# Stick-breaking attention of a hybrid decoder step: products of sigmoids by a scan, instead of log sums by matmuls

## The reference, cut to what matters

```python
z = jnp.einsum('bqhd,bkhd->bhqk', q, k, preferred_element_type=jnp.float32) * (SB_HEAD_DIM ** -0.5)
z = z + sb_bias.astype(jnp.float32)[None, :, None, None]
causal = k_pos[None, :] < q_pos[:, None]
log_keep = jnp.where(causal, jax.nn.log_sigmoid(-z), 0.0)
log_a = jax.nn.log_sigmoid(z) + lax.cumsum(log_keep, axis=3, reverse=True) - log_keep
a = jnp.where(causal, jnp.exp(log_a), 0.0)
return jnp.einsum('bhqk,bkhd->bqhd', a, v.astype(jnp.float32)).astype(v.dtype)
```

## Time and profile before

| | |
|---|---|
| median of 3 runs | 1183.52 us (1182.88 to 1184.49) |
| the profiled execution | 1182.75 us, its span 1181.0 us |
| TensorE matmuls busy | 1104.3 us, 94% of the span |
| VectorE, ScalarE, GpSimd busy | 523.8, 326.2, 130.0 us |
| mean granted TensorE clock | 0.974 of full speed |

### The profile page before, as it was taken

The page is one execution under the profiler, slowest core; times in us unless marked ns, Lnnn a source line. Parts: engine busy times, 40 slices in busy tenths (PEclk is TensorE's granted clock), DMA queues, the critical chain, the costliest instruction groups (busy, mean ns, idle before and its releaser), DMA issues.

```text
span 1181.0 us, 15790 instructions
## 1 busy us (share of the span) xinstructions
PE 1104.3 (94%) x6499; PEld 698.6 (59%) x6499; DVE 523.8 (44%) x733; ACT 326.2 (28%) x444; POOL 130.0 (11%) x179
## 2 busy tenths in 40 slices
PE   6999999999989999999998299999999999999996
PEld 5999977988667767799545233333333333333332
DVE  5222234886644333443122524444444555554445
ACT  5323211355368676633112011110011111111100
POOL 0000000013201322100000101111111111111110
PEclk9999899999989999999999589999999999999998
DMA  5622222554511322274414679999999999999941
GB/s 183 249 90 91 66 78 74 196 185 164 188 54 45 99 72 90 73 277 169 165 39 177 250 300 421 427 426 425 429 426 426 425 426 426 426 426 428 425 177 73
DMA packets 50067, 282.99 MB, mean 240 GB/s; under 512 B 6242, under 2 KB 6514, under 8 KB 29524
## 3 DMA queue, kind: packets, MB, share of 16 engines
q1 hardware_dynamic: 41188, 254.78, 53.7%
q0 software_dynamic: 6048, 20.98, 5.3%
q10 hardware_dynamic: 2768, 6.33, 1.5%
HBM read 274.56 MB, written 7.48 MB: 239 GB/s over the span
## 4 chain that ended last, share of the span: by engine, by line
PE 87%; DVE 6%; ACT 2%; DMA 2%; issue 1%; SPq 0%; DVEq 0%; POOL 0%; ACTq 0%; POOLq 0%
PE acc_all L746 25%; PE acc_all L1214 19%; PE acc_all L1228 10%; PE acc_all L876 5%; PE acc_all L1124 5%; PE acc_all L1239 5%; PE acc_all L725 4%; PE acc_all L807 2%; PE acc_all L988 2%; PE acc_all L1002 2%; PE acc_all L1242 2%; PE acc_all L1007 1%; PE acc_all L926 1%; DMA vals<-in_cache_mem_v 1%; DVE gate_h L2120 1%
## 5 line engine op out<-in xcount | busy, mean ns | idle before, releaser
L746 PE MATMUL acc_all<-xn_hi,w_hi 128*128 128x260 f32 x832 | 174.2, 291 | 10.6 <-DVE gate_sb L1822 6.0
L746 PE MATMUL acc_all<-xn_hi,w_lo 128*128 128x260 f32 x832 | 168.8, 285 | 0.0
L746 PE MATMUL acc_all<-xn_lo,w_hi 128*128 128x260 f32 x832 | 168.6, 285 | 0.0
L2131 DVE TENSOR_TENSOR x<-x,acc_all 128x1024 f32<-128x1024 f32 x128 | 152.6, 1215 | 1.8 <-PE acc_all L1239 0.9
L746 PEld LDWEIGHTS acc_all<-xn_hi,w_hi 128*128 128x128 f32 x832 | 130.2, 191 | 18.5 <-issue 17.1
L746 PEld LDWEIGHTS acc_all<-xn_lo,w_hi 128*128 128x128 f32 x832 | 129.9, 191 | 0.0
L746 PEld LDWEIGHTS acc_all<-xn_hi,w_lo 128*128 128x128 f32 x832 | 129.6, 190 | 0.0
L688 POOL TENSOR_SCALAR spread<-tok_row,slots 128x560 fp32r<-128x560 f32 x32 | 54.0, 1686 | 405.3 <-PE acc_all L1242 405.2
L1666 DVE TENSOR_TENSOR w_lo<-w_raw,w_hi 128x1024 fp32r<-128x1024 f32 x52 | 63.4, 1222 | 63.4 <-ACT w_hi L1353 63.2
L1597 ACT ACTIVATE gate_h<-acc_all 128x256 f32<-128x256 f32 x32 | 12.3, 383 | 260.3 <-PE acc_all L725 260.3
L2115 DVE COPY up_sb<-acc_all 128x512 f32<-128x512 f32 x32 | 22.1, 692 | 133.7 <-PE acc_all L1215 133.7
(11 more groups left out here) (355 smaller groups left out, 1886.2 us busy)
## 6 DMA issues: line engine op xcount, KB each, us to landing
w_a<-in_w SPq DMA_DIRECT2D x44, 1024.0 KB, 12.9
w_b<-in_w SPq DMA_DIRECT2D x44, 1024.0 KB, 13.2
w_c<-in_w SPq DMA_DIRECT2D x40, 1024.0 KB, 13.0
w_raw<-in_w_in SPq DMA_DIRECT2D x52, 512.0 KB, 3.6
w_a<-in_w SPq DMA_DIRECT2D x11, 2048.0 KB, 14.4
w_b<-in_w SPq DMA_DIRECT2D x11, 2048.0 KB, 13.9
w_c<-in_w SPq DMA_DIRECT2D x10, 2048.0 KB, 14.3
w_br<-in_w_branch SPq DMA_DIRECT2D x24, 256.0 KB, 4.4
```

The lines of the kernel that those rows point to most:

```text
L746: mm = pe.matmul(out[:, a, :], w[:, slot, k, :], x[:, k, a * HALF_TOK:(a + 1) * HALF_TOK], start=first, stop=last)
L2131: dve.tensor_tensor(x1[:, t, :], x1[:, t, :], bank(2 * pair, 2), ALU.add).then_inc(back_ok, 1)
```

## The change

Scores now stand with queries on partitions and keys along the free axis, two heads per pair: head 2p on the upper 64 rows of the array, head 2p+1 on the lower. ScalarE makes keep = sigmoid(-z) and beta = sigmoid(z) straight from the scores. GpSimd sets the masked part of a diagonal block to 1 in keep and to 0 in beta. VectorE's scan replaces keep by its running product from the last key backwards, in place, through a reversed pattern; beta is multiplied with keep shifted by one key. That is the weight, but turned the wrong way for `values`, so TensorE transposes its 20 blocks per pair, and ScalarE copies them to `a_sb`. Work is done once per pair: scores at the end of an odd step, scans in the even step, transposes in the odd step. Step 0's gate product moves ahead of the scores of pair 0, into banks 0 and 1, and the split of the cross-attention output goes in pieces. On VectorE `rest_chunk` moves behind `merge`.

```diff
-            def suffix_sums(h):
...
+            def scores(pair):
+
+                for r, t in Z_ORDER:
+                    at_col = SCORE_N * r + Z_AT[r][t]
+                    if (r, t) == Z_ORDER[-1]:
+                        pe.wait_ge(z_ps, 2 * pair + 1)
+                    rr = slice(HD * r, HD * (r + 1))
+                    mm = pe.matmul(acc_all[:, at_col:at_col + (t + 1) * P], proj[rr, Q0 + pair, tok(t)],
+                                   proj[rr, K0 + pair, 0:(t + 1) * P], start=True, stop=True, skip_group_check=True)
...
+            def turn_weights(pair):
...
+                pe.wait_ge(a_ok, 2 * pair + 2)
+                blocks(1, pieces[0:2])
+                blocks(0, pieces).then_inc(at_ps, 1)
+                blocks(1, pieces[2:]).then_inc(at_ps, 1)
...
+            gate(0, 0)
             turn_probs(2 * XH - 1)
...
+            scores(0)
...
             for h in range(HEADS):
+                pair, second = divmod(h, 2)
                 n = KD + h
...
+                if h >= 1:
                     pe.wait_ge(term_ok, h)
...
+                    gate(h, 6)
+                if second:
+                    turn_weights(pair)
+                elif pair >= 1:
+                    values(pair - 1)
...
+                if second and pair + 1 < HEADS // 2:
+                    pe.wait_ge(at_sb, 2 * pair + 2)
+                    scores(pair + 1)
...
+            def survivals(pair):
+
+                act.wait_ge(z_ps, 2 * pair + 2)
+                for tile, done, bias, sign in ((keep, keep_ok, nbias_bc, -1.0), (beta, beta_ok, sbias_bc, 1.0)):
+                    for r in range(2):
+                        h = 2 * pair + r
+                        act.activation(tile[:, r, :], acc_all[:, SCORE_N * r:SCORE_N * (r + 1)], ACT.Sigmoid,
+                                       bias=bias[:, h:h + 1], scale=sign * SB_SCALE).then_inc(done, 1)
...
+            def runs(pair):
+                for r in range(2):
+                    dve.wait_ge(keep_cut, 4 * (2 * pair + r + 1))
+                    for t in range(NT - 1):
+                        run = keep[:, r, seg(r, t)][:, ::-1]
+                        dve.tensor_tensor_scan(out=run, data0=run, data1=ones[:, 0:1].to_broadcast([P, (t + 1) * P]),
+                                               initial=1.0, op0=ALU.mult, op1=ALU.mult).then_inc(run_ok, 1)
+
+            def weigh(pair):
+                for r in range(2):
+                    dve.wait_ge(beta_cut, 4 * (2 * pair + r + 1))
+                    dve.wait_ge(run_ok, 4 * (2 * pair + r + 1))
+                    dve.tensor_tensor(beta[:, r, 0:SCORE_N - 1], beta[:, r, 0:SCORE_N - 1], keep[:, r, 1:SCORE_N],
+                                      ALU.mult).then_inc(a_ok, 1)
...
                 rest_branch(n, n % RING, 1)
...
+                if not second:
+                    runs(pair)
+                    weigh(pair)
...
+                if h != 6:
+                    merge(n, merged[:, h, :], acc_pair(6))
+                rest_chunk(IN_CHUNKS + n + 2)
```

More of the change, by code:

```diff
@@ L386, in build, with seg, cut @@
         ZM_AT, PMT_AT, SUMS_AT = 0, 256, 0
[L388 to L394, removed]
+        def seg(r, t, first=0, n=None):
+            at_col = Z_AT[r][t] + first
+            return slice(at_col, at_col + ((t + 1) * P if n is None else n))
+        def cut(pool, pair, tile, ready, fill, done):
+            for r in range(2):
+                pool.wait_ge(ready, 2 * pair + r + 1)
+                for t in range(NT - 1):
+                    v = tile[:, r, seg(r, t, t * P, P)]
+                    pool.affine_select(out=v, in_=v, compare_op=ALU.is_gt, fill=fill, base=0,
+                                       pattern=[[-1, P]], channel_multiplier=1).then_inc(done, 1)
         block = ctx.enter_context(nc.Block())
@@ L628, in _ @@
                 load_key(n)
[L629 to L640, removed]
+            for pair in range(HEADS // 2):
+                cut(pool, pair, keep, keep_ok, 1.0, keep_cut)
+                cut(pool, pair, beta, beta_ok, 0.0, beta_cut)
+                for b in ((0, 1), (2, 3, 4, 5), (6, 7), ())[pair]:
+                    load_val(b)
             pool.wait_ge(wo_ps, 2 * NT)
@@ L980, in _ @@
                 point(2 * n + 1)
[L983 to L991, removed]
@@ L993, in suffix_sums, with gate @@
-            def suffix_sums(h):
[L995 to L1010, removed]
+            def gate(h, pair):
+                pe.wait_ge(split_lo, IN_CHUNKS + KD + h + 1)
+                three_pass((KD + h) % RING, acc_pair(pair)).then_inc(gt_ps, 1)
@@ new lines, in turn_weights, with blocks @@
+            def turn_weights(pair):
+                def blocks(r, pieces):
+                    for kb, t in pieces:
+                        at_col = SCORE_N * r + SCORE_AT[kb] + (t - kb) * P
+                        mm = turn(acc_all[:, at_col:at_col + P], beta[:, r, seg(r, t, kb * P, P)], P)
+                    return mm
+                pieces = [(kb, t) for kb in range(NT - 1) for t in range(kb, NT - 1)]
+                pe.wait_ge(a_ok, 2 * pair + 2)
+                blocks(1, pieces[0:2])
+                blocks(0, pieces).then_inc(at_ps, 1)
+                blocks(1, pieces[2:]).then_inc(at_ps, 1)
@@ L1511, in _ @@
+            act.wait_ge(dot_ok, 2 * NB)
             for h in range(HEADS):
+                pair, second = divmod(h, 2)
                 n = KD + h
                 if h >= 1:
-                    split_chunk(IN_CHUNKS + n + 2)
                     act.wait_ge(br_ps, n)
                     split_branch(n, n % RING, 1, 16 * (n // RING + 1))
-                if h == 1:
+                if not second:
+                    survivals(pair)
+                if h >= 1:
+                    sigmoid(n, 6)
+                if h == 0:
+                    act.wait_ge(zs_ok, 1)
+                    link(act.activation(z_abs[:, :, :, :], zs[:, :, :, :], ACT.Abs))
+                    link(act.activation(z_abs[:, :, :, :], z_abs[:, :, :, :], ACT.Exp, scale=-1.0))
+                    act.activation(z_abs[:, :, :, :], z_abs[:, :, :, :], ACT.Ln, bias=1.0).then_inc(zsln_ok, 1)
+                if h == 2:
@@ L1520, in _ @@
                                    zs[:, :, :, :].rearrange("p j b h -> p (j b) h"), ACT.Exp).then_inc(as_ok, 1)
-                sigmoid(n, 6)
-                if h >= 2 and h % 2 == 0:
-                    stick_out(h // 2 - 1)
-                if h + 1 < HEADS:
-                    front(h + 1)
-                weights(h)
+                if second:
+                    turned_weights(pair)
+                elif pair >= 1:
+                    stick_out(pair - 1)
+                if h >= 1:
+                    split_chunk(IN_CHUNKS + n + 2)
             stick_out(HEADS // 2 - 1)
```

160 lines of the change are left out of this document (73 added, 87 removed).

## The result

The changed kernel takes 1147.26 us (median of 4 runs, 1144.99 to 1148.54), the kernel before 1183.2; the ratio is 0.9694, 95% interval 0.9681 to 0.9706. The prediction was 1147.3.

The account below looks back on a forecast made before the run. TensorE's own instructions were taken to bound the stage; summing gate products, scores, chain, clock loss and pairs brought the next stage's start from 499.16 to 463.0, 36.2 us earlier: 1147.3 us (1143 to 1151; wider range 1140 to 1158).

Parts of the forecast that it names:

- chain of pair 0: From pair 0's scores through sigmoid, cuts, scans, multiplications and merge to the next gate product: 11.8 us, mostly without cover.
- What goes: TensorE loses eight suffix sums of 4.54 us, 36.3 us; ScalarE's dropped passes lay under TensorE and are worth nothing.
- Transposes: On TensorE, 20 transposes of 128x128 come in per pair: 2.35 us, 9.4 us for four pairs.
- Scores: Two heads' score matmuls on TensorE's row halves overlap except for 256 columns: 2.8 us a pair.
- The scan: VectorE's eight scans over 2560 columns a pair take 5.2 us at 2.0 ns a column (3.0 at the lower value).
- Cuts and scans take turns: Rival: GpSimd's cuts and VectorE exclude each other, up to 3.1 us a pair, 9.5 in all, 1156.8 us; chance 0.17.
- The chain against its cover: Even steps: 11.8 us chain under 13.2 of TensorE work at pairs 1 and 2 (1.4 spare), 11.9 at pair 3.
- "unseen" loss: Rival: a wait not foreseen in steps 1 to 7 eats most of the gain, 1165 to 1183 us; chance 0.06.
- The clock: After pair 0's stall the next gate product runs at the low clock: loss 0 to 6.0 us, 2.8 taken.
- Cached values: Their loads after the sample values land at 20.6 to 21.7 us, TensorE needs them at 21.6; costed at nothing.
- The signs: Wrong if: idle over 1 us before pairs 1 and 2's odd gate products, scores near 4.7, stretched cuts, cached-value waits.
- The stall of pair 0: Gate product 0 was moved ahead of the scores, so TensorE stands still some 8 us before the second gate product.

Follow-up runs that it names:

- e1: The kernel before the change without the suffix-sum matmuls that multiply by ones, half of the sums' columns: 1175.24 us.
- e5: The changed kernel with all four score matmuls of one head, then all four of the other, instead of alternating: 1152.03 us.
- e6: The changed kernel with every scan done twice, the first time into a spare tile: 1175.30 us.
- e4: The changed kernel with VectorE's merge ahead of the scans in step 0: 1141.66 us.
- e2: The changed kernel with each scan replaced by a plain multiplication over the same columns: 1142.61 us.
- e3: The changed kernel without GpSimd's eight cuts of beta a pair: 1142.59 us.
- e9: The changed kernel measured again, unaltered, as a yardstick: 1146.89 us.
- e10: The changed kernel with step 0's merge ahead of the scans and, in step 1, the branch product ahead of the transposes: 1136.89 us.

## Why the prediction came true, step by step

The total was right because the forecast's mechanism was right in the main. That it was right to 0.1 us is luck: by the table, errors of -0.6, +1.5, -1.9, +0.3 and +0.7 us cancelled, and the runs of the changed kernel themselves lie between 1145.0 and 1148.5. Stretch by stretch, predicted and measured:

| stretch | predicted | measured |
| --- | --- | --- |
| gate product 0 to the end of the scores | 12.1 | 11.5 |
| chain of pair 0 | 11.8 | 13.3 |
| step 1 to the end of the next scores | 17.5 | 15.6 |
| pairs 1 and 2 | 58.5 | 58.8 |
| pair 3 to the next stage | 27.4 | 28.1 |
| stage | 127.3 | 127.4 |

- **What goes.** Right in sum, too simple in its reason. The trace before showed TensorE nearly always busy, and I took the other engines to have slack under it. e1 shows that the slack of ScalarE's pass was 1.1 us a head. That the chain ran through TensorE alone did not say how close the next wait was.
- **Transposes.** 2.18 us for 20 (2.35 forecast).
- **Scores.** 2.38 instead of 2.8. The 256 columns that I counted as unpaired cost nothing; e5 shows that the pairing is real. This is worth 0.4 four times.
- **The scan.** 6.41 instead of 5.2: the upper value of 2.0 ns a column was right to within 0.1 (2.1 by e6's rows, 5.3 us for 2560 columns). The term that was too small is the fixed cost of eight instructions, which were charged none: 6.05 us, where no more than a few cuts run beside them (e4), leaves 0.7 for it, and the cuts add up to 0.4. The Trainium skill (DVE: opcode table, instruction layouts, handler registers and perf-mode slots; Datapath and trigger behaviour) has the scan at half throughput, which gave an estimate of 5.9; the slopes agree, 2.1 ns a column against 1.0 for a multiplication (e2). The 1.16 ns that the forecast took for a plain pass holds that pass's fixed part, too.
- **Cuts and scans take turns.** The mechanism of this rival is there, its price is not. I gave it 3.1 us a pair; by e3 it is 1.0 for the cuts of beta (0.67 of wait and 0.2 to 0.3 of slower scans), and little more for those of keep (6.20 us of scans in e3, 6.05 in e4), since GpSimd is the one that waits and VectorE only meets the last cuts. The Trainium skill (SBUF — State Buffer; Terms) has the loser block fully, and the stretched cuts agree: 3.05 against 1.03.
- **The chain against its cover.** 13.2 to 13.3 us in place of 11.8, against a cover of 13.2 at pairs 1 and 2. The forecast's 1.4 us to spare were all used up, and e6 shows that nothing was left. No idle time came ahead of gate products 3 and 5, so the "unseen" loss did not arise, by a margin of about nothing. Pair 3 lacked 1.3, as its cover of 11.9 made it.
- **The clock.** 1.6 us lost on gate product 1 instead of 2.8 (7.62 against 6.0), 2.3 in e9. It was placed rightly.
- **Cached values.** I costed their loads at nothing, landing at 20.6 to 21.7 us with need at 21.6. They came late: 0.25 and 1.0 us (3.2 in e9). The first two issues took 1.31 and 1.45 us instead of 0.95, and transfers up to 6.5 to land. With no room in the reckoning it should have been a cost.
- **The signs.** Of the signs of being wrong, two came: the cuts were stretched beyond 0.3 us each (3.05 for four, 5.32 for eight), and steps 3 and 5 waited on cached values. Neither brought its rival's time: the cuts cost 1.0 us where 3.1 were feared, the waits 1.3 in all.
- **The stall of pair 0.** Rightly named and rightly laid to the order: e4 and e10 get 4.8 and 6.8 us of the stage back without touching the scans.

What stays open is why the loads of cached values and the clock behind the stall cost more in one execution of the same kernel than in another (e9).

## What to carry to other kernels

A busy engine in the chain that ended last does not say how near the second wait is: take a part of its work out and see whether the time follows. When a new long chain is laid under other work, count a fixed part for every instruction in it, and put ahead of it whatever others wait for and what does not need it (here the merge), since the stall costs its length and then the clock. A chain and a cover that agree to 0.1 us leave nothing to spare: whatever makes the chain longer comes into the time whole (e6).

## What the runs showed of the hardware

- GpSimd's cuts and VectorE's instructions with two SBUF operands take turns, plain multiplications as well as scans (e2), but unevenly: a cut beside a scan of 1.24 us took 1.20, eight cuts of 0.26 us took 5.32, while the scans grew only from 6.05 (in e4, where most cuts were done before) to 6.41.
- A scan in place on a reversed pattern costs 2.1 ns a column and, in its record, 0.17 us an instruction (records overlap a little), against 1.0 ns a column for a multiplication ((1.48 - 0.71)/760, and the earlier trace rows).
- Matmuls on 64 rows that alternate between the two halves take the time of half their columns (2560 in 2.38 us, one head's 1280 in 2.35); one head behind the other they take 3.77.
- What the low clock behind a stall costs differs between runs of one kernel: gate product 1 took 7.62 us in one profile of the changed kernel and 8.30 in the other, 6.0 being the full clock's.
